# Sixteen projection pieces beside block 0's expert groups, a first tile routed in three parts, and nine row buffers in a kernel that gathers experts

## The chip, the cores and the metric

The kernel runs on one core of one Trainium2 chip. The metric is the device time of one launch in microseconds (us). The engines are named as in the profile: PE (TensorE, matmul), PEld (its weight loads), DVE (VectorE), ACT (ScalarE), POOL (GpSimd) and SP (SyncE, which issues plain transfers). Sixteen DMA engines move data for the core. All values are float32.

## The reference, cut to what matters

A residual block over 1024 tokens of width 1024: two kinds of attention with projections, then a layer that picks, for every token, 128 of 16384 single-neuron experts and sums them.

```python
proj = rmsnorm(h, ln) @ w_in                 # qa, ka, va, qb, kb, vb
o_a = stick_breaking_attention(qa, ka, va)   # group A: 8 heads, all earlier tokens
o_b = sliding_window_sink_attention(rope(qb), rope(kb), vb, sinks)   # group B
h = h + concat(rmsnorm(o_a, sb_norm), rmsnorm(o_b, swa_norm)) @ w_out
t = rmsnorm(h, ln_ffn)
q = (t @ w_query).reshape(tokens, 8, 2, 64)            # 8 routing heads
s = einsum('thpd,hpnd->thpn', q, sub_keys)             # scores of 2 x 128 sub-keys
s1, i1 = top_k(s[:, :, 0], 16); s2, i2 = top_k(s[:, :, 1], 16)
top_s, pos = top_k(s1[..., :, None] + s2[..., None, :], 16)    # 16 experts of a head
g = softmax(top_s)
act = gelu(einsum('thkd,td->thk', expert_u[idx], t))
out = h + einsum('thk,thkd->td', g * act, expert_v[idx])       # then one last rmsnorm
```

## The kernel before, in words

The tokens are cut into eight tiles of 128 (NT). A tile t has a *routing part* (window attention, output projection, norm, query, key scores, top 16, which experts) and a *block* t, in which its experts are fetched and summed. A block has 128 gathers (K): gather k brings, for each of 128 tokens, one row of 2048 values (the expert's two vectors, 8 KB) into one of NB row buffers, `uv[:, slot, :]` in `r_uv`. Two gathers make a *group*; a block has 64 groups (NG). For a group, DVE forms two dot products (L1246), ACT takes their gelu (L898) and builds two scaled identities in place (L901), PE adds the rows into two banks of PSUM (L1577, eight matmul instructions of the profile for a group), and its last matmuls raise `rows_used`, which lets POOL issue the next gather into that buffer (L680).

Every engine works through its own list in order. What a list holds besides the groups is set by tables: `at` gives the group beside which each step of the next tile's routing stands, `at_own` the steps of the block's own tile, `at0` the steps of tile 0 before the first block. A *top* step finds the 16 best keys of both halves of one head (L1061 to L1073), *scores* and *numbers* lay out the candidates (L1136), a *pick* finds one head's 16 experts (L1061 to L1174), a *gate* makes the indices that POOL waits for (`idx_ready`, L1045), *routed* finishes the softmax that the first group of these heads waits for.

The *head* of the program (all before the first gather) holds the norm, the transposes, the value projections, and then the *pieces*: a piece is the projection of one weight chunk (a pair of heads of QA, KA or QB) for 256 tokens, 16 matmul instructions of the profile at L1345 in `sum_piece`; ACT takes it out of PSUM (L756, `keep_piece`), SP stores it in DRAM (`store_piece`). A QB piece is also *turned* by one more matmul (L1359) and roped by DVE (L978 to L980). There are 48 pieces; the head has 42 of them (NH), one to a step s, and between them tile 0's routing and the first twelve units of stick-breaking attention (`first_...`, steps 12 to 19). Pieces 26 to 41 stand after a gap (GAP), in which PE forms tile 0's queries (L1526) and key scores (L1534). The last six pieces stand beside groups 0 to 5 of block 0.

All pieces read the normalised input `xnT`, which lies where row buffers 0 to 3 are; buffers 0 and 1 open when the head's last piece is summed, buffers 2 and 3 after the last piece of all. So the list of slots uses six buffers for groups 0 to 8 and eight from there. The later units of stick-breaking attention (`late_...`) stand beside the groups of blocks 0 to 4 from group 28 on: scores, then four groups later `late_later` (L1375 to L1381), then `late_weigh` (L1388). Between them POOL adds up what the next unit subtracts (`late_add`, L642 and L644), in its own list between two gathers.

## Time and profile before

| | us |
|---|---|
| three runs | 3050.13, 3052.65, 3055.52 (median 3052.65) |
| span of the profiled execution, first to last instruction | 3048.5 |
| what lies around the span, against the median | 4.15 |
| first gather issued / last gather issued | 350.5 / 3019.3 |
| busy in the span: PE, DVE, ACT, POOL | 2245.9, 2188.7, 1151.6, 1317.4 |
| moved in the span | 1143.41 MB, of which the gathers 1073.81 MB |

The profile is of one execution. The page cuts the span into 40 slices of 76 us and gives for each the busy share of the engines in tenths, the mean busy share of the 16 DMA engines and the bytes per second that they moved. The views of stretches give the same for any stretch. Views in order of time give single instructions, with the idle time of the engine before them and what ended it.

### The profile page before, as it was taken

To read this page: it belongs to the slowest core of one execution; us is meant where nothing else is said; L and a number is where in the kernel's file an instruction comes from. 1 tells how busy PE (TensorE), PEld (TensorE's weight loads), DVE (VectorE), ACT (ScalarE), POOL (GpSimd) and SP (SyncE) were. 2 spreads that over 40 slices of the span, in tenths; PEclk is the share of its full clock that TensorE was granted. 3 is DMA by queue.
4 is the path that set the end of the run, shared out by engine and by line. 5 is a ranking of instruction groups with operands and counts; after the bars stand their busy time and mean duration, and the time that the engine had idled before them with its cause. 6 is when DMAs were issued, how large, how long until landed. Compare 5 with 4: busy or idle time off the path is not lost.

```text
span 3048.5 us, 29992 instructions
## 1 busy us (share of the span) xinstructions
PE 2245.9 (74%) x8606; PEld 913.2 (30%) x8606; DVE 2188.7 (72%) x5399; ACT 1151.6 (38%) x2656; POOL 1317.4 (43%) x1134
## 2 busy tenths in 40 slices
PE   8999887786777777776878678876755576555555
PEld 5677733221332123221332124222311132111111
DVE  2121867888788777887788778887777787776654
ACT  4142132774246432663367334753311322121111
POOL 1000144554455444554455544554444444444443
PEclk9999998898889788898899888988877898777777
DMA  3541599999999999999999999999999999999997
GB/s 121 184 129 41 173 388 417 409 407 418 415 418 402 418 413 418 408 415 412 417 406 411 411 416 418 407 398 419 416 415 421 413 404 419 415 420 410 420 420 319
DMA packets 198050, 1143.41 MB, mean 375 GB/s; under 512 B 23584, under 2 KB 55664, under 8 KB 66560
## 3 DMA queue, kind: packets, MB, share of 16 engines
q0 software_dynamic: 147456, 1073.81, 85.7%
q1 hardware_dynamic: 50432, 67.71, 6.6%
q8 instruction: 69, 1.13, 0.1%
q14 instruction: 93, 0.76, 0.1%
HBM read 1126.34 MB, written 15.07 MB: 374 GB/s over the span
## 4 chain that ended last, share of the span: by engine, by line
DMA 35%; PE 29%; DVE 18%; ACT 7%; issue 7%; POOL 4%; SPq 0%; POOLq 0%; ACTq 0%; DVEq 0%
DMA r_uv<-in_experts,r_wk 34%; PE ps L1577 13%; DVE r_uv L1246 8%; PE ps L1345 4%; POOL r_uv L680 4%; PE ps L1509 3%; PE ps L1300 3%; ACT r_uv L901 2%; PE ps L1526 1%; ACT L898 1%; PE ps L1375 1%; DVE r_wk L1173 1%; DVE r_wk L1171 1%; DVE r_wk L1174 1%; ACT r_wk L811 1%
## 5 line engine op out<-in xcount | busy, mean ns | idle before, releaser
L1577 PE MATMUL ps<-r_uv 128*64 128x512 f32 x4096 | 1293.0, 766 | 757.7 <-ACT r_uv L901 735.0
L680 POOL DMA_INDIRECT r_uv<-in_experts,r_wk x1024 | 1207.7, 1179 | 1488.9 <-PE ps L1577 1127.3
L1246 DVE CUSTOM_DVE_ANT_0 r_uv<-r_uv,hnrep 128x1024 f32<-128x1024 f32 x1024 | 1267.0, 1250 | 531.3 <-DMA r_uv<-in_experts,r_wk 516.8
L1577 PEld LDWEIGHTS ps<-r_uv 128*64 128x64 f32 x4096 | 299.1, 162 | 1556.2 <-ACT r_uv L901 1065.9
L898 ACT ACTIVATE r_wk<-r_wk 128x2 f32<-128x2 f32 x512 | 104.1, 203 | 1517.3 <-DVE r_wk L1246 1484.6
L901 ACT ACTIVATE r_uv<-gid,r_wk 128x64 f32<-128x64 f32 x684 | 200.6, 340 | 11.7 <-ACT r_wk L898 0.3
L898 ACT ACT_TABLE_LOAD x136 | 174.5, 1283 | 2.4
L702 ACT ACT_TABLE_LOAD x128 | 164.2, 1283 | 5.7 <-PE ps L1500 1.4
L1526 PEld LDWEIGHTS ps<-r_wk,r_wq 128*128 128x128 f32 x1024 | 124.5, 199 | 57.1 <-issue 57.1
L1526 PE MATMUL ps<-r_wk,r_wq 128*128 128x128 f32 x1024 | 135.4, 288 | 0.8 <-ACT r_wk L840 0.8
L1369 PE MATMUL ps<-r_wk 64*128 64x256 f32 (+2 forms) x384 | 112.3, 414 | 8.8 <-DMA r_wk<-lkv_dram 4.9
L1509 PE MATMUL ps<-r_wo,r_wk 128*128 128x512 f32 x256 | 117.6, 603 | 0.0
L1231 DVE TENSOR_TENSOR gid<-cst,r_wk 128x128 f32<-128x128 f32 x342 | 111.4, 326 | 0.2 <-DVE r_wk L1073 0.2
L1375 PE MATMUL ps<-r_wk,cst 128*128 128x512 f32 (+2 forms) x192 | 106.2, 636 | 5.4 <-POOL r_wk L644 3.0
L901 ACT ACTIVATE r_uv<-cst,r_wk 128x64 f32<-128x64 f32 x340 | 99.7, 340 | 5.8 <-ACT r_wk L898 0.2
L1345 PE MATMUL ps<-r_uv,hnrep 128*128 128x256 f32 x416 | 95.7, 385 | 0.0
L644 POOL TENSOR_TENSOR r_wk<-r_wk 128x512 f32<-128x512 f32 (+1 forms) x64 | 84.3, 1318 | 1.2 <-PE ps L1381 0.2
L1246 DVE DVE_READ_ACCUMULATOR2_ANT r_wk<- 128x1 f32 x1024 | 83.3, 81 | 0.0
L1345 PEld LDWEIGHTS ps<-r_uv,hnrep 128*128 128x128 f32 x416 | 79.1, 192 | 13.7 <-issue 3.0
L1300 PE MATMUL ps<-r_wq,r_wo 128*128 128x512 f32 (+3 forms) x288 | 80.1, 436 | 0.0
L642 POOL COPY r_wk<-r_wk 128x256 f32<-128x256 f32 x32 | 16.9, 529 | 137.9 <-PE ps L1378 121.3
L1381 PE MATMUL ps<-r_wk,cst 128*128 128x512 f32 (+2 forms) x160 | 75.9, 556 | 0.0
(152 smaller groups left out, 2083.1 us busy)
## 6 DMA issues: line engine op xcount, KB each, us to landing
r_uv<-in_experts,r_wk POOLq DMA_INDIRECT x1024
r_wk<-lkv_dram SPq DMA_DIRECT2D x72, 128.0 KB
hnrep<-in_w_chunks SPq DMA_DIRECT2D x14, 512.0 KB, 3.8
r_uv<-in_x SPq DMA_DIRECT2D x8, 512.0 KB, 3.3
r_wo<-in_w_out SPq DMA_DIRECT2D x8, 512.0 KB, 5.2
r_wk<-in_x SPq DMA_DIRECT2D x8, 512.0 KB
r_wq<-in_w_query SPq DMA_DIRECT2D x8, 512.0 KB, 4.2
result<-h2cur SPq DMA_DIRECT2D x8, 512.0 KB
```

What stands on the lines that cost most here:

```text
L680: g.indirect_dma_start(uv[:, SLOT[G], :], None, experts, bass.IndirectOffsetOnAxis(idx[b % 2][:, k:k + 1], 0)).then_inc(rows_in[SLOT[G]], 16)
L702: a.preload_act_table_set("natural_log_exp_and_others")
L898: link(a.activation(actv[:, GRP * n:GRP * n + GRP], actv[:, GRP * n:GRP * n + GRP], ACT.Gelu))
L901: a.activation(uv[:, SLOT[K * b + k], 0:HALF], gid[(NG * b + n) % 3][:, k % GRP, :], ACT.Copy, scale=actv[:, k:k + 1]).then_inc(diag_ready, 1)
L1246: v.tensor_tensor_reduce(uv[:, slot, 0:D], uv[:, slot, 0:D], hnrep[:, k % GRP, :], 1.0, 0.0, ALU.mult, ALU.add, actv[:, k:k + 1]).then_inc ...
L1300: last = t_.matmul(ps[0:rows, bank, 0:w], xTc[:, u, c, 0:rows], wv[:, c, c0:c0 + w], start=c == 0, stop=c == DC - 1)
L1345: last = t_.matmul(ps[:, place, 0:GW], w[:, c, :], xnT[:, tb, c, :], start=c == 0, stop=c == DC - 1)
L1369: t_.matmul(bank(u, r, c0)[:, h, :], k[rows, 0:r], q[rows, c0:GW], start=h == 0, stop=False, skip_group_check=True).then_inc((lz_half, lz_ ...
L1375: last = t_.matmul(bank(u, r, c0), negtri[0:r, 0:r], sp[0:r, :, c0:GW], start=False, stop=not own and rest == GW, skip_group_check=True)
L1509: last = t_.matmul(ps[:, 2 + i, :], (oa, ob)[i // 2][:, c, :], wout[:, 4 * (i // 2) + c, 512 * (i % 2):512 * (i % 2) + 512], start=c == 0, ...
L1526: last = t_.matmul(ps[:, 4 + h // 4, P * (h % 4):P * (h % 4) + P], wq[:, c, P * h:P * h + P], hnT[:, c, :], start=c == 0, stop=c == DC - 1)
L1577: last = t_.matmul(ps[HALF * j:HALF * j + HALF, i, :], uv[:, slot, 0:HALF], uv[:, slot, D + 512 * i:D + 512 * i + 512], start=n == 0, stop ...
```

## The change

- NH falls from 42 to 32: sixteen pieces (all of QA and KA for tokens 512 to 1023) stand beside groups 0, 1, 4, 5, 8, 9, 20, 21, 33, 34, 38, 39, 43, 44, 48 and 49 of block 0. They share one new weight buffer of 4 KB a partition, `stream_chunk`, loaded eight times, seven of these within block 0; before, the last three chunks were loaded once each, ahead of the first gather.
- In the head the twelve QB pieces of tokens 256 to 1023 now come ahead of the gap, in steps 12 to 23, beside the first attention units; they were behind it. Six pieces are left behind the gap, where there were sixteen.
- Tile 0 is routed in three parts: heads 0 and 1, heads 2 and 3, heads 4 to 7. The first gathers wait for two heads where they waited for four. Top steps 3 to 5 and picks 2 and 3 move from the head to block 0 (`own_first`); top steps 6 and 7 stood there before. Routing steps of tile 1 stand up to four groups later (`at_first`).
- Nine row buffers. Buffers 8, 0, 4, 5, 6, 7, 1 serve the first 52 groups; 2 and 3 join at group 52 (WIDE). The 12 KB a partition that the ninth buffer and `stream_chunk` take come from the descriptor scratch of POOL's transfers, cut from 16 KB (the default) to 4 KB.
- PSUM banks of turned and weighed pieces are shared, so some waits are new: a turn waits for the rope of the one before, and the seventh attention unit's weighing waits for two copies of the first pairs (`oa_first`).
- POOL's `late_add` of a unit that starts at group G stands behind the gathers of group G+8 in block 0 as before, and of G+9 in blocks 1 to 4.

```diff
-NB = 8
+NB = 9
-GAP = (26, 32)
+GAP = (26, 29)
+STREAM_GROUPS = (0, 1, 4, 5, 8, 9, 20, 21, 33, 34, 38, 39, 43, 44, 48, 49)
+PARTS = [((0, 2), (2, 4), (4, 8))] + [((0, 4), (4, 8))] * (NT - 1)
+WIDE = 52
+RING = [8, 0, 4, 5, 6, 7, 1]
+for _G in range(NT * K):
+    if _G == GRP * WIDE:
+        _free = [2, 3] + _free
+    SLOT.append(_free.pop(0))
+    _free.append(SLOT[-1])
...
-            opens = {1: (q_roped, len(TURNED)), 2: (proj_summed, NH), NARROW: (proj_summed, NP)}
+            opens = {0: (proj_summed, NQ), 6: (q_roped, len(TURNED)), 1: (proj_summed, NH), 2: (proj_summed, NP)}
+
+            def add_group(b, late, u):
+
+                return min(NG - 1, LATE_AT[late][u] + LATER + (4 if b == 0 else 5))
...
-            at0 = {8: "exp", 10: "pT", 11: "ob", 21: "oa", 22: "r2", 24: "h2sq", 26: "hnT", 43: "gexp"}
+            at0 = {8: "exp", 10: "pT", 11: "ob", 21: "oa", 22: "r2", 24: "h2sq", 26: "hnT", NS: ("gexp", 0)}
...
+            own_first = {0: [("top", 3)], 1: [("scores", 1), ("numbers", 1)], 2: [("pick", 2)], 4: [("pick", 3)],
+                         5: [("gate", 1)], 6: [("top", 4)], 7: [("routed", 1), ("top", 5)], 9: [("top", 6), ("top", 7)],
...
             def first_weigh(u):
...
+                if u == len(FIRST_UNITS) // 2:
+
+                    gate(pe, "pe", oa_first, 2)
...
-                    if b == 0 and n < NP - NH:
-                        sum_piece(NH + n)
+                    if b == 0 and n in STREAM_AT:
+                        sum_piece(STREAM_AT[n])
...
-    nc = bacc.Bacc("TRN2", target_bir_lowering=False, num_devices=1)
+    nc = bacc.Bacc("TRN2", target_bir_lowering=False, num_devices=1, dynamic_dma_scratch_size=4096)
```

Where the change moves instructions, three places. First PE around tile 0's queries and key scores (L1526 and L1534 before are L1577 and L1588 after; L1345 is L1388, a turn L1359 is L1402). Before:

```order
L1509 MATMUL ps<-r_wo,r_wk 128x512 x8
L1345 MATMUL ps<-r_uv,hnrep 128x256 x32
L1516 MATMUL ps<-cst,r_wk 128x128 x8
L1526 MATMUL ps<-r_wk,r_wq 128x128 x64
L1534 MATMUL ps<-keysT,r_wk 128x128 x16
L1345 MATMUL ps<-r_uv,hnrep 128x256 x8
L1345 MATMUL ps<-r_uv,h2cur 128x256 x16
L1359 MATMUL ps<-fnb,cst 128x256
```

and after:

```order
L1388 MATMUL ps<-r_uv,h2cur 128x256 x8
L1567 MATMUL ps<-cst,r_wk 128x128 x8
L1577 MATMUL ps<-r_wk,r_wq 128x128 x40
L1588 MATMUL ps<-keysT,r_wk 128x128 x8
L1577 MATMUL ps<-r_wk,r_wq 128x128 x24
L1588 MATMUL ps<-keysT,r_wk 128x128 x8
L1388 MATMUL ps<-r_uv,hnrep 128x256 x16
L1388 MATMUL ps<-r_uv,h2cur 128x256 x8
L1388 MATMUL ps<-r_uv,hnrep 128x256 x16
L1388 MATMUL ps<-r_uv,h2cur 128x256 x8
L1634 MATMUL ps<-r_uv 64x512 x4
```

The key scores of heads 0 to 3 now come after five of eight queries, and behind the key scores stand six pieces and no turn ahead of the first expert group (L1634).

Second, POOL's gathers at the start of block 0, with what they wait for (L680 before, L715 after). Before:

```order
L680 DMA r_uv<-in_experts,r_wk 128x2048 [waits side_out,v_out,lw_used,idx_ready,rows_used]
L680 DMA r_uv<-in_experts,r_wk 128x2048 [waits rows_used]
L680 DMA r_uv<-in_experts,r_wk 128x2048 [waits q_roped,rows_used]
L680 DMA r_uv<-in_experts,r_wk 128x2048 [waits rows_used]
L680 DMA r_uv<-in_experts,r_wk 128x2048 [waits proj_summed,rows_used]
L680 DMA r_uv<-in_experts,r_wk 128x2048 [waits rows_used] x13
```

and after:

```order
L715 DMA r_uv<-in_experts,r_wk 128x2048 [waits side_out,v_out,lw_used,idx_ready]
L715 DMA r_uv<-in_experts,r_wk 128x2048 [waits proj_summed]
L715 DMA r_uv<-in_experts,r_wk 128x2048 x2
L715 DMA r_uv<-in_experts,r_wk 128x2048 [waits q_roped]
L715 DMA r_uv<-in_experts,r_wk 128x2048
L715 DMA r_uv<-in_experts,r_wk 128x2048 [waits proj_summed]
L715 DMA r_uv<-in_experts,r_wk 128x2048 [waits rows_used] x25
```

Seven gathers stand ahead of the first that waits for a used buffer, and their waits on pieces are on ones that come early, but for the seventh, which waits for the head's last piece.

Third, PE at groups 32 to 34 of block 0 (an expert group is L1577 before and L1634 after; late units are L1369 to L1381 before, L1412 to L1424 after). Before:

```order
L1577 MATMUL ps<-r_uv 64x512 x4
L1375 MATMUL ps<-r_wk,cst 128x2x128
L1378 MATMUL ps<-cst 128x2x128
L1369 MATMUL ps<-r_wk 128x256
L1577 MATMUL ps<-r_uv 64x512 x4
L1375 MATMUL ps<-r_wk,cst 128x512
L1378 MATMUL ps<-cst 128x2x128
L1381 MATMUL ps<-r_wk,cst 128x2x128
L1369 MATMUL ps<-r_wk 16x256
L1577 MATMUL ps<-r_uv 64x512 x4
```

and after:

```order
L1634 MATMUL ps<-r_uv 64x512 x4
L1418 MATMUL ps<-r_wk,cst 128x2x128
L1421 MATMUL ps<-cst 128x2x128
L1412 MATMUL ps<-r_wk 128x256
L1634 MATMUL ps<-r_uv 64x512 x4
L1388 MATMUL ps<-r_uv,stream_chunk 128x256 x8
L1418 MATMUL ps<-r_wk,cst 128x512
L1421 MATMUL ps<-cst 128x2x128
L1424 MATMUL ps<-r_wk,cst 128x2x128
L1412 MATMUL ps<-r_wk 16x256
L1634 MATMUL ps<-r_uv 64x512 x4
L1388 MATMUL ps<-r_uv,stream_chunk 128x256 x8
```

A piece stands between an expert group and the late unit's matmuls at eight of the groups from 33 to 49.

## Rows read from the trace of the kernel before

**Rows 1.** The page, slices of the span: DMA busy tenths, bytes moved

```profile
DMA  3541599999999999999999999999999999999997
GB/s 121 184 129 41 173 388 417 409 407 418 415 418 402 418 413 418 408 415 412 417 406 411 411 416 418 407 398 419 416 415 421 413 404 419 415 420 410 420 420 319
```

**Rows 2.** The page, queues: packets, MB, share of 16 engines' span

```profile
q0 software_dynamic: 147456, 1073.81, 85.7%
q1 hardware_dynamic: 50432, 67.71, 6.6%
```

**Rows 3.** Stretches: length, engines' busy us, granted clock, DMA share, GB/s

```profile
350.00:434.00 84.00, 68.26 (x291) 40.45 (x290) 61.89 (x184) 21.91 (x67) 32.08 (x28) 0.92 0.92 348
434.00:543.00 109.00, 85.28 (x391) 39.53 (x391) 88.01 (x233) 37.70 (x94) 51.18 (x42) 0.90 1.01 418
543.00:634.00 91.00, 73.70 (x268) 24.52 (x266) 75.58 (x168) 65.18 (x117) 51.98 (x44) 0.89 1.00 402
617.00:3030.00 2413.00, 1698.25 (x6178) 576.33 (x6177) 1871.01 (x4527) 937.13 (x2195) 1179.11 (x1003) 0.84 1.01 413
...
580.00:590.00 10.00, 9.86 (x42) 3.15 (x40) 8.25 (x22) 7.83 (x17) 6.02 (x5) 0.99 0.93 360
...
3020.00:3030.00 10.00, 5.20 (x16) 1.17 (x16) 5.34 (x10) 1.60 (x7) 0.21 (x1) 0.83 0.89 368
```

**Rows 4.** PE in the head, in order of time: start, length, instructions

```profile
125.25 3.62 PE L1345 MATMUL ps<-r_uv,h2cur 128*128 128x256 f32 x16
...
129.14 3.62 PE L1345 MATMUL ps<-r_uv,hnrep 128*128 128x256 f32 x16
...
222.03 0.66 PE L1388 MATMUL ps<-r_uv 128*64 128x128 f32 x8
...
267.11 13.98 PE L1345 MATMUL ps<-r_uv,hnrep 128*128 128x256 f32 x64
...
280.92 1.04 PE L1516 MATMUL ps<-cst,r_wk 128*128 128x128 f32 x8
...
282.79 7.38 PE L1526 MATMUL ps<-r_wk,r_wq 128*128 128x128 f32 x64 [0.83 <-ACT r_wk L840]
...
297.24 2.82 PE L1534 MATMUL ps<-keysT,r_wk 64*128 64x128 f32 x32
```

**Rows 5.** DVE and POOL from tile 0's first top step to the first gather

```profile
299.72 0.49 DVE L1061 MAX8 r_wk<-r_wk 128x8 f32<-128x128 f32 x2 [20.01 <-ACT r_wk L849]
...
302.73 0.49 DVE L1061 MAX8 r_wk<-r_wk 128x8 f32<-128x128 f32 x2
...
316.90 0.78 DVE L1136 TENSOR_TENSOR r_wk<-r_wk 128x64 f32<-128x64 f32 x7
...
341.06 0.42 DVE L978 TENSOR_TENSOR r_uv<-ps,r_uv 128x256 f32<-128x256 f32 x1
...
342.42 0.21 DVE L1061 MAX8 r_wk<-r_wk 128x8 f32<-128x50 f32 x1
...
346.21 0.99 DVE L1174 TENSOR_REDUCE r_wk<-r_wk 128x16 f32<-128x800 f32 x1
...
348.74 0.74 DVE L1045 CAST r_wk<-r_wk 64x32 uint32<-64x32 f32 x4
...
350.53 1.20 POOL L680 DMA_INDIRECT r_uv<-in_experts,r_wk  x1 [122.95 <-issue]
```

**Rows 6.** The first groups: DVE's dots, PE's sums, POOL's next issue

```profile
363.00 2.79 DVE L1054 COPY hnrep<-r_wk 64x1024 f32<-64x1024 f32 x4
365.83 1.22 DVE L1246 CUSTOM_DVE_ANT_0 r_uv<-r_uv,hnrep 128x1024 f32<-128x1024 f32 x1
...
377.65 1.22 DVE L1246 CUSTOM_DVE_ANT_0 r_uv<-r_uv,hnrep 128x1024 f32<-128x1024 f32 x1
...
379.94 0.28 DVE L1231 TENSOR_TENSOR gid<-cst,r_wk 128x128 f32<-128x128 f32 x1
...
381.61 1.94 PE L1577 MATMUL ps<-r_uv 128*64 128x512 f32 x8
...
384.35 0.94 POOL L680 DMA_INDIRECT r_uv<-in_experts,r_wk  x1 [2.27 <-PE ps L1577]
```

**Rows 7.** POOL's gathers: ns least, median, most; first and last start

```profile
L680 POOL DMA_INDIRECT r_uv<-in_experts,r_wk x1024: 932/949/2612, 350.5 to 3019.3; - x171
```

More of the change, by code:

```diff
@@ L683, in gathers_of @@
                     if late is not None and k % GRP == GRP - 1:
[L684 to L685 removed]
+                        for u in range(len(LATE[late][1])):
+                            if add_group(b, late, u) == k // GRP:
+                                late_add(b, late, u)
             for b in range(NT):
@@ L1529, in tile_step @@
                 elif step[0] == "keys":
+                    if t == 1 and step[1]:
+                        gate(pe, "pe", proj_kept, NH + sum(n < 29 for n in STREAM_GROUPS))
                     pe.wait_ge(qT_kept, 2 * t + 1 + step[1])
```

266 lines of the change are left out of this document (144 added, 122 removed).

## Prediction, on record before the changed kernel ran

> **What bounds the kernel now.** I read the slices first. From the sixth slice on the DMA line shows 9, and 400 to 420 GB/s are moved [rows 1]. The queues say by whom: the gathers' packets fill 85.7% of sixteen engines' span, 0.857 x 3048.5 = 2613 us, or 2.55 us for each of 1024 gathers, and the plain transfers 6.6%, 201 us [rows 2]. The stretches show that nothing else counts in between: from 617 to 3030 the DMA share is 1.01, while PE is busy 1698 of 2413 us and DVE 1871 [rows 3]. So the time is the moment of the first gather, plus what the DMA engines must move after it, plus the time in which they have nothing to do, plus a short end. Of such holes there are few. Cut into 260 stretches of 10 us from 430 to 3030, the trace has 21 with a share under 1.00 (the first and the last in [rows 3]); what they lack against the usual 1.015 adds up to 10.7 us. The stretch from 350 to 434 has a share of 0.92, so 84 x 0.095 = 8 us of holes. Everything that the change can win lies in the first 350 us and in these 19 us.
>
> **The head.** Three edits move the first gather. (1) The twelve QB pieces now come ahead of tile 0's queries, and each brings a turn. A piece with a turn takes 129.14 - 125.25 = 3.89 us, one without 13.98 / 4 = 3.50 [rows 4]; 12 x 0.4 = 4.7 us on PE, which has no idle time there. The ropes lie on DVE beside it. (2) The weighing at 222.03 [rows 4] now waits for two pairs of copies, which stand on DVE behind the rope of the turn just done: a rope takes 342.42 - 341.06 = 1.4 us [rows 5], the copies about 0.9, so 2.5 us (0 to 4) in which PE and all behind it wait. Together the transpose at 280.92 moves to 288.1. (3) The first key scores come after five queries, not eight: 282.79 to 297.24 is 14.45 us for eight [rows 4], so 5.4 us less. They start at 297.2 + 7.2 - 5.4 = 299.0, and the first top step 2.5 us later, as now (299.72 after 297.24), at 301.5. From there DVE alone decides: two top steps of 3.0 (299.72 to 302.73), scores and numbers of two heads some 2.3 (0.78 for the four heads' scores), two picks of 4.8 (342.42 to the end of the reduce at 347.2), the indices 0.9, and 1.0 from there to the issue [rows 5]: 6.0 + 2.3 + 9.6 + 0.9 + 1.0 = 19.8. The eight ropes that stood between these steps are gone. First gather at **321.3** instead of 350.5: **29 us won** (25 to 33).
>
> **The first stretch.** What is late next is the first dot. PE finishes the second half of queries and key scores at about 308 and six pieces of 3.5 us at 329; ACT takes the last piece out and forms the gates' exponential only then (both stand at the end of its head), so DVE, done with top step 2 at 323, waits to 329.6. With 1.4 us for the gates and 2.8 for the copies of the normed rows [rows 6] the first dot starts at about 334, 12.6 us after the first issue; now it is 15.3. Seven gathers are under way by then, 17.9 us of moving, to about 341; the first buffers come free at 334 + 2.5 for two dots + 4.4 (379.94 to 384.35) [rows 6] = 341, and the next gather moves some 2 us later. After this DVE sets the pace: ten groups need 10 x 2.5 of dots and identities (377.65 to 380.15, [rows 6]), top steps 3 to 7 15.0, picks 2 and 3 9.6, and mask, candidates, gates and a copy some 9, together 59 us. DMA needs 20 x 2.55 = 51 plus about 7 for stores, three weight chunks and a window. That is level, with jitter: I take 8 us of holes, as now (3 to 18), so **0**.
>
> **More bytes behind the first gather.** Seven loads of 0.524 MB and some seven more stores of 0.131 MB: 4.6 MB. The gathers pay 2613 / 1073.8 = 2.43 us for a MB, the plain queue 201 / 67.7 = 2.97 [rows 2]; small stores are the dearer kind. 11 to 14, **12 us**, all on the path.
>
> **Seven buffers until group 52, and PE beside them.** Now eight serve from group 9. With eight, 434 to 543 has a share of 1.01 [rows 3]; a buffer less takes one gather, 2.55 us, from the lead. I take 5 us (0 to 10). Groups 33 to 49 are the tight place. PE is busy 73.7 of 91 us from 543 to 634 [rows 3], which are about these groups; eight pieces add 8 x 3.5 = 28, to 102. DMA has 91 plus 8 for its own share of the pieces: 99. Also, `late_add` of a unit that starts at group G comes behind a gather that now waits for group G+5's sums, one group later than with eight buffers; the next unit's matmuls, beside that same group if it started at G+1, then wait for an issue and an addition, about 2.5 us. Where a piece stands between (groups 33, 39, 48) it hides this, at 36, 42 and 45 nothing does. So PE needs 102 to 109 against 99: another 5 us (2 to 15). Together **10 us** (2 to 25).
>
> **Nine buffers from group 52 on.** They can give back holes only, some 9 of the 10.7 us, as the rest is the end of the gathers and what block 0 has. A lead longer by 2.55 us closes most holes of 1 us or less: **6 us won** (0 to 9). The later additions of blocks 1 to 4 fall on a PE that idles 30% of the time [rows 3]: nothing.
>
> **The smaller scratch.** What shows in the trace: 147456 packets for 1024 gathers [rows 2], 144 each, nine to an engine, and never more than nine gathers open, 81. The Trainium skill (DMA: Bandwidth & Descriptors, "The descriptor swizzle") has nine read and nine write descriptors per engine for such a transfer and 16 bytes for one ("Terms"); 4096 / 16 = 256, room for 28 gathers, is an estimate from that page, and by it the cut costs nothing. No run here shows that size yet. I take 0 (0 to 9, the price of slower issues below).
>
> **The sum.** -29 + 0 + 12 + 10 - 6 = -13 us. Span 3048.5 - 13 = 3035.5; the median of the runs is 4.15 above the span, so 3039.5, **3039 us**.
>
> **Rivals.**
> - *Block 0 keeps up.* DVE and PE are not the limit anywhere and the ninth buffer closes all holes: -29 + 12 - 4 - 9 = -30, 3022 us. For it: the DMA work of the new pieces widens every group. Against it: DVE's 59 against 58.
> - *The gain is given back in block 0.* The first stretch runs 3 us worse and groups 28 to 52 cost 20: -29 + 3 + 12 + 20 - 6 = 0, 3052 us. For it: PE's 102 to 109 against 99, in lists worked in order with a shorter lead.
> - *Slower: PE at its lower clock.* The mechanism is the pieces at half speed. The granted clock is 0.90 and 0.89 of full in 434 to 634 [rows 3], that is, part of the time PE is at 1.2 GHz, after waits for ACT. If the pieces fall into that, each takes 7 us: eight are 56, PE needs 130 in groups 33 to 49 against 99, 31 us lost; -29 + 12 + 31 + 5 - 6 = +13, 3065 us. It turns slower from about 25 us lost in block 0, six of the eight pieces at the low level. Against it: a PE with more to do waits less.
> - *The ninth buffer does nothing.* The holes come from something that a longer lead doesn't reach: 3045 us.
> - *POOL is slowed by DVE.* Issues take 949 ns in the median, up to 2612 [rows 7], 1179.11 us busy for 1003 of them [rows 3], so 0.23 us each over the median, hidden by the lead. With an empty queue, as in the first 40 gathers, the lengthening is on the path: 40 x 0.23 = 9 us, 3048 us. The Trainium skill (SBUF — State Buffer, "Who interferes with whom") gives a rule for this: some copies on DVE lock POOL out of the port with which it writes descriptors. By that rule moving top steps and copies beside gathers lengthens issues; that some are longer agrees, that it costs time is not seen.
>
> **How the numbers follow.** The forecast has 0.50, block 0 keeping up 0.13, given back 0.17, slower 0.10, the idle ninth buffer 0.06, POOL 0.04. A measurement of this kernel can tell about 0.2%, 6 us, from no change. Faster by more: nearly all of the forecast, block 0 keeping up, and most of the idle ninth buffer, 0.68. Within: given back, POOL and the edges, 0.21. Slower: 0.11. The range reaches from the best case, 3022, to just over the given-back one, 3054; the bounds of the terms (25 to 33, 11 to 14, 2 to 25, 0 to 9, 3 to 18 for 8) add up to about the same.
>
> **What would show it.** The first gather at 321 (318 to 326), the first dot 12 to 13 us behind it, DVE idle ahead of it for 6 us. A DMA share of 0.9 in the first 84 us behind the first gather, near 1.01 and at worst 0.95 in groups 28 to 52, and hardly a stretch of 10 us under 0.99 after group 52. PE busy over 90% in groups 33 to 49, with waits for POOL at L1418. Wrong I would be if the first gather were later than 326, if PE's clock fell under 0.85 beside the pieces, or if the gathers' rate behind group 52 changed at all apart from the holes.

## The result, and the profile after

The changed kernel takes **3090.3 us** (median of four runs, 3088.7 to 3094.9), the kernel before, beside it, 3054.1 us. The ratio is 1.0123, with a 95% interval of 1.0111 to 1.0135: slower by 1.2%, where 3039 us and a small gain were forecast. The profiled execution has a span of 3089.9 us, 41.4 us more than the 3048.5 of before; it is the one that is taken apart here. The medians lie 36.2 us apart. Around the span of the changed kernel lie 1.8 us (3091.7 against 3089.9), so of the 4.15 us of the kernel before some 2 are that its profiled execution was quicker than its median.

The page of the changed kernel, first the DMA share and the bytes by slice, then the two queues, then the line of PE's `late_later` matmuls (name, count, busy us and mean ns, idle us ahead of them and who ended it):

```profile
DMA  3532799889999999999999999999999999999997
GB/s 119 185 120 64 298 404 401 329 349 419 418 418 417 417 413 418 402 418 416 411 384 380 371 418 418 362 367 414 418 420 419 419 404 419 416 420 410 419 420 319
...
q0 software_dynamic: 147456, 1073.81, 84.9%
q1 hardware_dynamic: 51584, 71.90, 6.9%
...
L1418 PE MATMUL ps<-r_wk,cst 128*128 128x512 f32 (+2 forms) x192 | 114.2, 680 | 79.3 <-POOL r_wk L675 73.3
```

and the same line of the kernel before:

```profile
L1375 PE MATMUL ps<-r_wk,cst 128*128 128x512 f32 (+2 forms) x192 | 106.2, 636 | 5.4 <-POOL r_wk L644 3.0
```

Against [rows 1], where the GB/s line stands between 398 and 421 from the seventh slice to the last but one, there are three dips: 329 and 349 (540 to 695 us, the late groups of block 0), 384, 380, 371 (1545 to 1776 us, block 3) and 362, 367 (1931 to 2085 us, block 4). Between them the rate is what it was. And a wait has grown from 3.0 us: PE idles 79.3 us ahead of L1418, 73.3 of it for POOL L675. L675 is the addition in `late_add`, L1418 the first matmul of `late_later`.

The same as stretches (length, busy us of each engine, granted clock, DMA share, GB/s): the first groups behind the first dot, the middle of block 0, its late groups, and the halves of blocks 3 and 4 with late units.

```profile
344.00:424.00 80.00, 59.15 (x244) 30.10 (x246) 75.38 (x238) 23.28 (x72) 29.54 (x27) 0.88 1.00 400
424.00:545.00 121.00, 101.51 (x472) 51.80 (x469) 98.90 (x275) 51.04 (x112) 53.88 (x44) 0.94 0.99 398
545.00:660.00 115.00, 100.95 (x380) 45.15 (x380) 72.34 (x160) 68.17 (x125) 50.18 (x46) 0.90 0.86 317
1557.00:1745.00 188.00, 139.22 (x478) 44.33 (x476) 148.79 (x353) 120.10 (x214) 104.17 (x84) 0.87 0.94 369
1911.00:2098.00 187.00, 144.80 (x466) 45.55 (x466) 143.36 (x344) 117.21 (x208) 98.97 (x83) 0.84 0.95 372
```

PE is busy 0.84 of the second stretch, 0.88 of the third and 0.74 and 0.77 of the last two; no engine is full, and yet the DMA engines have holes. A *hole* is counted here and below from the packets: the share of the sixteen engines that moves nothing, added up over a stretch and given in us.

When gathers number 0, 16 and so on have their last packet in, after against before, worked out from both traces' packets (two gathers make a group, 128 a block):

| gather | before, us | after, us | difference | with late_add back (e_add34) | head mended too (e_head34) |
|---|---|---|---|---|---|
| 0 | 356.6 | 336.2 | -20.5 | -17.9 | -31.7 |
| 16 | 412.3 | 383.7 | -28.5 | -25.5 | -38.9 |
| 64 | 538.3 | 519.0 | -19.3 | -13.5 | -28.1 |
| 104 | 646.4 | 658.7 | +12.2 | -2.2 | -15.0 |
| 128 | 707.7 | 721.4 | +13.6 | -0.8 | -13.7 |
| 448 | 1546.1 | 1557.0 | +10.9 | -3.8 | -17.1 |
| 512 | 1716.6 | 1744.5 | +27.9 | -4.0 | -15.5 |
| 576 | 1883.4 | 1911.4 | +28.1 | -4.6 | -15.7 |
| 640 | 2054.6 | 2097.3 | +42.7 | -5.0 | -19.1 |
| 1023 | 3032.6 | 3075.8 | +43.1 | -1.2 | -16.2 |

So 17 us are lost in the second half of block 3 (gathers 448 to 512), 15 in that of block 4, 42 in block 0 behind gather 16; 28.5 are won up to there and 3 in blocks 1 and 2, and 43 are left. These halves are where the late units start, in blocks 0, 3 and 4 two in three groups; blocks 1 and 2, whose units start two groups apart, lose nothing. PE's waits for POOL at L1418 lie in the same places: 14.9 us in block 0, 5.5 in blocks 1 and 2, 58.7 in blocks 3 and 4.

What a late unit waits for, from the changed kernel's trace of block 3, PE and POOL in order of time (start, length, line, what ended the idle time ahead):

```profile
1611.64 1.94 PE L1634 MATMUL ps<-r_uv 128*64 128x512 f32 x8
...
1614.69 1.67 POOL L715 DMA_INDIRECT r_uv<-in_experts,r_wk  x1 [2.70 <-issue]
1616.38 1.27 POOL L675 TENSOR_TENSOR r_wk<-r_wk 128x512 f32<-128x512 f32 x1
...
1617.79 2.04 PE L1418 MATMUL ps<-r_wk,cst 128*128 128x512 f32 x2 [4.22 <-POOL r_wk L675]
1617.81 1.75 POOL L715 DMA_INDIRECT r_uv<-in_experts,r_wk  x1 [0.16 <-issue]
...
1619.63 1.91 PE L1424 MATMUL ps<-r_wk,cst 128*128 128x512 f32 x2
```

PE ends a group's sums at 1613.6, and only then may POOL issue the gather which stands ahead of the addition in its list (it waits for `rows_used`, which these sums raise). The issue starts at 1614.7 and takes 1.67 us, the addition 1.27, and PE, with the next unit's `late_later` at its head, stands idle for 4.22 us. The next group's sums, which would free the next buffers, are queued behind it. And the two groups of matmuls that follow take 2.04 and 1.91 us, where the unit at 1608.5, behind a wait of 0.2 us, takes 1.10 and 1.02: the granted clock from 1617 to 1620 is 0.50, the lower level of 1.2 GHz. It isn't so behind every wait. Of the 18 waits for POOL at L1418 that are longer than 3 us, 15 are followed by matmuls that run at the lower clock at least in part, three (3.2, 3.4 and 3.6 us) by ones at the full clock; of the 19 shorter waits, one is followed by slower ones.

The head. PE in order of time, changed kernel:

```profile
222.87 3.72 PE L1388 MATMUL ps<-r_uv,hnrep 128*128 128x256 f32 x16
...
229.91 1.12 PE L1431 MATMUL ps<-r_uv 128*64 128x128 f32 x8 [2.89 <-DVE r_wk L1065]
...
230.96 2.08 PE L1418 MATMUL ps<-r_wk,cst 128*128 128x512 f32 x2
...
237.44 3.72 PE L1388 MATMUL ps<-r_uv,hnrep 128*128 128x256 f32 x16
...
296.17 1.09 PE L1567 MATMUL ps<-cst,r_wk 128*128 128x128 f32 x8 [2.15 <-DVE r_wk L1161]
298.10 10.80 PE L1577 MATMUL ps<-r_wk,r_wq 128*128 128x128 f32 x80 [0.83 <-ACT r_wk L876]
308.82 1.71 PE L1588 MATMUL ps<-keysT,r_wk 64*128 64x128 f32 x16
```

The transpose stands at 296.2, not at the 288.1 of the prediction; the first gather was issued at 330.5.

### The profile page after: what moved, and what is told of

Same layout as the page of the kernel before. It is cut to its first block, busy times and chain, and to the rows that moved or that the text cites. A ratio compares the mean times of both kernels' runs of the same rounds, so it can differ in the third digit from the quotient of the medians.

```text
span 3089.9 us, 30050 instructions
## 1 busy us (share of the span) xinstructions
PE 2238.4 (72%) x8606; PEld 913.6 (30%) x8606; DVE 2183.6 (71%) x5428; ACT 1152.0 (37%) x2659; POOL 1332.8 (43%) x1134
## 3 DMA queue, kind: packets, MB, share of 16 engines
q8 instruction: 69, 1.13, 0.1%
## 4 chain that ended last, share of the span: by engine, by line
PE 36%; DMA 33%; DVE 14%; ACT 7%; issue 6%; POOL 4%; SPq 0%; POOLq 0%; ACTq 0%; DVEq 0%
DMA r_uv<-in_experts,r_wk 32%; PE ps L1634 15%; DVE r_uv L1285 6%; PE ps L1388 5%; POOL r_uv L715 3%; PE ps L1560 3%; PE ps L1337 3%; PE ps L1418 2%; ACT r_uv L940 2%; PE ps L1577 2%; PE ps L1424 2%; POOL r_wk L675 1%; PE ps L1412 1%; ACT L937 1%; ACT r_wk L847 1%
## 5 line engine op out<-in xcount | busy, mean ns | idle before, releaser
L715 POOL DMA_INDIRECT r_uv<-in_experts,r_wk x1024 | 1230.5, 1202 | 1506.8 <-PE ps L1634 1197.2
L1634 PE MATMUL ps<-r_uv 128*64 128x512 f32 x4096 | 1256.9, 747 | 733.9 <-ACT r_uv L940 712.9
L1634 PEld LDWEIGHTS ps<-r_uv 128*64 128x64 f32 x4096 | 294.3, 160 | 1524.3 <-ACT r_uv L940 1033.9
L1418 PE MATMUL ps<-r_wk,cst 128*128 128x512 f32 (+2 forms) x192 | 114.2, 680 | 79.3 <-POOL r_wk L675 73.3
L1577 PEld LDWEIGHTS ps<-r_wk,r_wq 128*128 128x128 f32 x1024 | 123.9, 199 | 47.7 <-issue 47.6
L1577 PE MATMUL ps<-r_wk,r_wq 128*128 128x128 f32 x1024 | 134.1, 288 | 0.8 <-ACT r_wk L876 0.8
L1412 PE MATMUL ps<-r_wk 64*128 64x256 f32 (+2 forms) x384 | 113.1, 419 | 3.5 <-DMA r_wk<-lkv_dram 2.4
L841 ACT ACTIVATE r_wk<-ps 128x512 f32<-128x512 f32 (+2 forms) x84 | 47.5, 565 | 111.0 <-PE ps L1424 108.7
L1424 PE MATMUL ps<-r_wk,cst 128*128 128x512 f32 (+2 forms) x160 | 88.2, 637 | 0.0
L1388 PE MATMUL ps<-r_uv,hnrep 128*128 128x256 f32 x352 | 82.8, 391 | 0.0
L675 POOL TENSOR_TENSOR r_wk<-r_wk 128x512 f32<-128x512 f32 (+1 forms) x64 | 76.5, 1195 | 1.2 <-PE ps L1424 0.3
## 6 DMA issues: line engine op xcount, KB each, us to landing
r_uv<-in_experts,r_wk POOLq DMA_INDIRECT x1024, 14.1
```

Source lines behind the costliest of these rows:

```text
L715: g.indirect_dma_start(uv[:, SLOT[G], :], None, experts, bass.IndirectOffsetOnAxis(idx[b % 2][:, k:k + 1], 0)).then_inc(rows_in[SLOT[G]], 16)
L1388: last = t_.matmul(sums, w[:, c, :], xnT[:, tb, c, :], start=c == 0, stop=c == DC - 1)
L1418: last = t_.matmul(bank(u, r, c0), negtri[0:r, 0:r], sp[0:r, :, c0:GW], start=False, stop=not own and rest == GW, skip_group_check=True)
L1424: last = t_.matmul(bank(u, r, rest), negones[:, 0:r], acc[:, :, rest:GW], start=False, stop=True, skip_group_check=True)
L1577: last = t_.matmul(ps[:, 4 + h // 4, P * (h % 4):P * (h % 4) + P], wq[:, c, P * h:P * h + P], hnT[:, c, :], start=c == 0, stop=c == DC - 1)
L1634: last = t_.matmul(ps[HALF * j:HALF * j + HALF, i, :], uv[:, slot, 0:HALF], uv[:, slot, D + 512 * i:D + 512 * i + 512], start=n == 0, stop ...
```

## Experiments

Each kernel ran beside the kernel before, and the ratio to it stands with each time. A single trace can lie some us off the median of its kernel (e_head34: 3032.4 in the profiled execution, 3040.2 in the median), so small differences go by the times, places by the traces. The ratio isn't that of the two medians. Where a price is given as a range, one end is the difference of the medians and the other that of the ratios.

**e_add4: late_add back in its place in blocks 1 to 4.**

```
-                return min(NG - 1, LATE_AT[late][u] + LATER + (4 if b == 0 else 5))
+                return min(NG - 1, LATE_AT[late][u] + LATER + 4)
```

> The changed kernel, and only in blocks 1 to 4 each late_add stands one group earlier again (behind the gathers of group G+8, where it waits for the sums of group G+4, as with eight buffers); block 0 is as in the changed kernel. Theory A (the later place of late_add is what costs: PE's next late_later, at L1418, waits for a gather issue and an addition on POOL): the 17 us that gathers 384 to 512 lost and the 15 us that gathers 512 to 640 lost come back, 3090 - 32 = 3058 us, between 3052 and 3064; the waits of PE for POOL L675 fall from 73 us to about 35; block 0 still ends some 13 us late. Theory B (the blocks 3 and 4 lose it by the ninth buffer itself or by the descriptor scratch of 4 KB, PE's waits are a sign and not the cause): 3085 to 3092 us.

Measured: 3062.1 us, ratio 1.0023 (1.0014 to 1.0033), 28 us under the changed kernel by the medians, 31 by the ratios. The waits for POOL fell to

```profile
PE ps L1418 <- POOL r_wk L675: 12.7, 6, 3.3
```

(us in all, times, longest), and the stretch that took 188 us takes 176, at 395 instead of 369 GB/s:

```profile
1557.00:1733.00 176.00, 136.55 (x482) 43.56 (x481) 143.43 (x353) 121.22 (x215) 103.60 (x85) 0.90 0.99 395
```

One digit of one line is worth 28 of the 36 us. Theory B falls. But the waits fell to 12.7 us where 35 were expected: block 0, which is left as it was, holds 14.9 us of them in the changed kernel, not half of the 73.

**e_add34: the same in block 0.**

```
+                return min(NG - 1, LATE_AT[late][u] + LATER + (3 if b == 0 and LATE_AT[late][u] + LATER + 3 < WIDE else 4))
```

> As e_add4, and in block 0, where seven buffers serve, late_add stands one group earlier as well (behind the gathers of group G+7, from which they wait for group G+4; for the few units whose place would lie in or past group 52 the place stays). Theory A: block 0 lost 39 us between gathers 40 and 104; the waits for POOL at L1418 in block 0 are about half of the 73 us, and when they go PE has 8 x 3.5 = 28 us more to do than before in groups 33 to 49 but no more; I expect 20 us (10 to 30) back, so 3058 - 20 = 3038 us, between 3028 and 3050. Rival C (block 0 loses by the load of the pieces on PE and by the buffer less, not by the waits): no more than 5 us under e_add4.

Measured: 3047.9 us, ratio 0.9966 (0.9951 to 0.9981): 14 us less than e_add4 by the medians, 17 by the ratios, 16 between the two traces, and the kernel is now faster than the one before. Rival C had no more than 5. The expected 20 (10 to 30) rested on half of the 73 us of waits; it came near with 14.9 us, because in block 0 a wait costs about its whole length. The late groups of block 0 then run with PE nearly full and at full clock:

```profile
545.00:645.00 100.00, 94.25 (x398) 44.18 (x394) 75.41 (x168) 71.02 (x129) 51.75 (x47) 1.00 0.97 382
```

**b_add_later: the kernel before, with late_add one group later.**

```
-                        for u in late_units(late, k // GRP - NB // GRP - LATER):
-                            late_add(b, late, u)
+                        for u in range(len(LATE[late][1])):
+                            if min(NG - 1, LATE_AT[late][u] + LATER + 5) == k // GRP:
+                                late_add(b, late, u)
```

> The kernel before, with one edit: each late_add stands one group later, behind the gathers of group G+9, where with eight buffers it waits for the sums of group G+5. Theory A: PE waits for POOL in the units one group apart, in blocks 3 and 4 as in the changed kernel (+32 us), in block 0 without the pieces less than there (+5 to +20): 3054 + 32 + 12 = 3098 us, between 3080 and 3110, with about 60 us of waits at L1375 for L644. Theory B: within 5 us of 3054.

Measured: 3171.0 us, ratio 1.0391 (1.0359 to 1.0423). The direction is as theory A has it, the size is not: +117 us, not +44. The trace of this kernel has

```profile
PE ps L1376 <- POOL r_wk L644: 163.1, 58, 5.6
...
PE ps L1376 <- POOL r_wk L642: 17.0, 6, 3.7
```

180 us of waits, and block 3 loses 43 us, block 4 40, block 0 31. With eight buffers the gather ahead of the addition waits for the second gather of group G+5, with nine for the first, and the lead that can absorb the wait is a gather shorter. This account of the size is argued, no run tries it alone. What a us of wait costs differs by block:

| PE's waits for POOL, us, and what the stretch loses | block 0 | blocks 1 and 2 | blocks 3 and 4 |
|---|---|---|---|
| changed kernel | 14.9, loses 14 to 17 | 5.5, loses nothing | 58.7, loses 28 to 32 |
| b_add_later | 42, loses 31 | 40, loses 3 | 98, loses 83 |

In blocks 1 and 2, whose units start two groups apart, even 40 us of waits cost next to nothing; where units start one group apart they cost half of their length or more.

**e_one34: e_add34 with one eighth of the streamed pieces' matmuls.**

```
-                for c in range(DC):
+                deep = DC if i < NH else 1
+                for c in range(deep):
...
-                                     stop=c == DC - 1)
+                                     stop=c == deep - 1)
```

> As e_add34, and the sixteen streamed projection pieces do one of their eight matmuls each, so that queries and keys of tokens 512 to 1023 are wrong; all loads, copies, ropes and stores stay. It takes 16 x 7 x 0.43 = 48 us off PE, 24 us of it in groups 33 to 49. If PE's load is what block 0 still loses by (rival C), it ends 10 to 20 us under e_add34, about 3025 us; if the waits for late_add were all (theory A), it ends within 4 us of e_add34.

Measured: 3045.2 us, ratio 0.9965 (0.9951 to 0.9979), against 0.9966. 48 us of work taken off PE move next to nothing (2.7 us by the medians, 0.3 by the ratios): by itself, PE's load was not what block 0 still lost by.

**e_head34: e_add34 with three places on DVE and ACT changed in the head.**

```
-            at0 = {8: "exp", 10: "pT", 11: "ob", 21: "oa", 22: "r2", 24: "h2sq", 26: "hnT", NS: ("gexp", 0)}
+            at0 = {8: "exp", 10: "pT", 11: "ob", 21: "oa", 22: "r2", 23: "h2sq", 26: "hnT", NS: ("gexp", 0)}
...
-            at0 = {7: "mask", 9: "norm", 10: "pT", 23: "r2", 24: "h2", 25: "hn", 28: ("top", 0), 29: ("top", 1),
+            at0 = {7: "mask", 9: "norm", 10: "pT", 22: "r2", 25: "hn", 28: ("top", 0), 29: ("top", 1),
...
+                if s == 23:
+                    tile_step("h2", 0)
                 if s - 2 in PIECE_AT and PIECES[PIECE_AT[s - 2]][0] == QB:
                     rope_piece(PIECE_AT[s - 2])
...
-                if c in (5, 8):
-                    dve.wait_ge(lw_used, len(FIRST_UNITS) * (c - 2) // 6)
-                    first_out(2 * (c // 3) - 2)
-                    first_out(2 * (c // 3) - 1)
+                if c in (4, 8):
+                    dve.wait_ge(lw_used, len(FIRST_UNITS) * (c // 4) // 2)
+                    first_out(2 * (c // 4) - 2)
+                    first_out(2 * (c // 4) - 1)
```

> The kernel of the run e_add34, and in the head: the two copies of first_out that a weighing waits for stand on DVE one step earlier, ahead of the softplus pair; the polish r2 and the step h2 of tile 0 stand ahead of the rope of the turn that PE only reaches behind the output projection; ACT squares h2 one step earlier. The trace of the changed kernel has PE idle 2.9 us before 229.91 for these copies, about 1.9 us more by the lower granted clock right behind it, and 2.15 us before 296.17 for hn. Theory D (these DVE places are two thirds of the excess of the head over the predicted 288.1): the transpose hnT starts 6 to 7 us earlier, near 290, the first gather near 325, and the time is 3048 - 6 = 3042 us. Rival E (PE has no slack behind, the turns themselves cost): within 2 us of e_add34, the first gather at 330.

Measured: 3040.2 us, ratio 0.9960 (0.9945 to 0.9974). PE in this kernel's head:

```profile
219.90 3.72 PE L1390 MATMUL ps<-r_uv,hnrep 128*128 128x256 f32 x16
...
223.98 0.66 PE L1433 MATMUL ps<-r_uv 128*64 128x128 f32 x8
...
229.91 3.72 PE L1390 MATMUL ps<-r_uv,hnrep 128*128 128x256 f32 x16
...
286.61 1.09 PE L1569 MATMUL ps<-cst,r_wk 128*128 128x128 f32 x8
288.53 9.17 PE L1579 MATMUL ps<-r_wk,r_wq 128*128 128x128 f32 x80 [0.83 <-ACT r_wk L876]
297.63 1.71 PE L1590 MATMUL ps<-keysT,r_wk 64*128 64x128 f32 x16
```

The waits are gone, the weighing takes 0.66 us instead of 1.12, from one piece to the next it is 10.0 us instead of 14.6, five queries take 9.17 instead of 10.80, and the transpose stands at 286.6. The first gather was issued at 319.3. That is more than the 6 to 7 us of theory D, and it is not luck of one trace: the six kernels with this head have it at 318.9 to 323.5 (319.3, 319.2, 318.9, 320.4, 321.4, 323.5), the six with the changed kernel's head at 327.0 to 333.0. In the time of the whole, though, the medians are 8 us apart and the ratios 0.0006, with intervals that overlap. That the first gather is some 10 us sooner is shown; that the kernel is faster by as much is not. With the additions back and the head mended the kernel takes what was forecast for the change, 3039 us, and that is luck in part: by the trace the head gives 31 us (29 predicted), the first stretch 7 (0), block 0 takes 25 (22), and what comes behind it gives 2 (6).

**e_fo34: only first_out's place.** The edit is the last hunk above.

> The kernel of the run e_add34, and of the head's edits only the first: the copies of first_out for which a weighing waits stand one step earlier on DVE, ahead of the softplus pair. In three runs with the wait the piece behind it began 16.0 us after the piece before it (222.85 to 238.85), in e_head34 10.0 us. Theory D: the idle 2.9 us and the lower granted clock that follows it are one cause, so this edit alone gives 4.5 to 6 us, and the piece stands 10 us behind: 3048 - 5 = 3043 us, hnT near 291 to 292. Rival: the rest of e_head34's gain was h2's place, and this run gives 2 to 3 us: 3045.5 us.

Measured: 3043.7 us, ratio 0.9965 (0.9954 to 0.9976). The piece stands 10.0 us behind the one before it (223.58, 233.59), the transpose at 292.3, the first gather at 325.0. So a wait of 2.9 us had cost 4.6 to 6 us, with the lower clock behind it (0.61 granted from 229 to 233 in the changed kernel, 1.00 from 223 to 230 in e_head34), and the place of r2 and h2 gives the other 5.7 us at the transpose.

**e_wide54, e_wide64: when the chunk's two buffers join.** `WIDE = 52` becomes 54 (on e_add34) and 64 (on e_head34).

> The kernel of the run e_add34, with the two buffers of the chunk joining at group 54 instead of 52. In e_add34 the gather of group 52 was issued 14.7 us behind that of group 51, waiting 6.3 us for PE L1388, the last streamed piece (it stands in group 49), and the DMA share from 620 to 640 was 0.86. Theory F: the join at 52 is a wait of its own, about 3 us: 3045 us and no such gap. Rival: seven buffers for four gathers more cost the same; 3048 us.

Measured: 3045.6 us, ratio 0.9974 (0.9965 to 0.9983), against 0.9966: the gap at the join is gone from the trace (no holes between gathers 96 and 112, where e_add34 has 3.4 us). The medians lie 2 us apart and the ratios the other way, so the time is the same; the trace has its holes a few groups earlier.

> The kernel of the run e_head34, with seven buffers for all of block 0: the two of the chunk join at group 64, not 52. It prices seven buffers. The recorded prediction takes 5 us (0 to 10) for the whole of block 0's narrow part. Theory: with late_add in its place seven serve at a share of 0.97 to 1.0, so twelve groups more cost 2 us and the wait of 6 us at the join goes: within 3 us of 3040. Rival (seven buffers are what makes block 0 slow, 24 gathers more at the 2.66 us of gathers 40 to 104 against 2.59 of eight): 3 to 6 us slower, 3045.

Measured: 3040.7 us, ratio 0.9962 (0.9949 to 0.9976), against 0.9960. Gathers 104 to 128 go at 2.69 us with seven buffers and 2.61 with nine, 2 us in all.

**e_eight34: e_add34 with eight buffers from group 52.** `_free = [2, 3] + _free` becomes `_free = [2] + _free`.

> The kernel of the run e_add34, but one buffer, not two, joins at group 52: eight buffers serve from there, as in the kernel before. From gather 128 to the last e_add34 took 2324.5 us and the kernel before 2324.9, with 12.8 and 11.4 us of DMA holes: by these the ninth buffer gives nothing once late_add is back in its place, and this run is within 3 us of e_add34 (3045 to 3051). By the recorded prediction (the ninth buffer closes holes, 6 us) it is 3054 us.

Measured: 3049.8 us, ratio 0.9988 (0.9978 to 0.9997), against 0.9966. From gather 128 to the last its trace takes 2326.3 us, that of e_add34 2324.5. The ninth buffer is worth 2 us by the trace and the medians, 7 by the ratios; the prediction's 6 lies within.

**b_scratch: the kernel before with the smaller descriptor scratch.** `dynamic_dma_scratch_size=4096` is added, nothing else.

> The kernel before, with the descriptor scratch of 4 KB and nothing else. The recorded prediction has 0 (0 to 9) for it: 3054 us, with issues of 949 ns in the median as before. If the smaller scratch made issues longer or wait, the backlog of the gathers hides up to about 6 us of it each, and the time is up to 3063 us.

Measured: 3053.8 us, ratio 1.0002 (0.9993 to 1.0011). The gathers' issues (least, median, most ns, first and last start) are as in [rows 7]:

```profile
L680 POOL DMA_INDIRECT r_uv<-in_experts,r_wk x1024: 932/960/2808, 352.0 to 3025.9; - x171
```

The scratch costs nothing here. The Trainium skill (DMA: Bandwidth & Descriptors, "The descriptor swizzle") led to the same answer by its count of descriptors.

**e_noload and e_light: the new loads, and loads and matmuls together.** Both are e_head34 without the seven loads; e_light has also the edit of e_one34.

```
                             gate(e, "sp", proj_summed, i + 1)
-                            load_chunk(c + 1)
...
-                    gate(pe, "pe", stream_in, 16 * (c - TAIL + 1))
+                    gate(pe, "pe", stream_in, 16)
```

> The kernel of the run e_head34, without the seven loads of weight chunks behind the first gather: all sixteen streamed pieces are formed with the first chunk's weights, so queries and keys of tokens 512 to 1023 are wrong. SP still waits where it did. It prices the term of the new bytes: by the recorded prediction 4.6 MB cost 12 us, of which the loads are 3.67 MB, some 9.5 us: 3040 - 9.5 = 3030.5. In the traces block 0 loses 17 to 18 us between gathers 16 and 128 beside the holes; if the loads hit thin queues, they are worth more, 14 us, 3026. If they run in the holes, less than 5 us.

Measured: 3035.9 us, ratio 0.9938 (0.9925 to 0.9952): 4 to 7 us for 3.67 MB, where the prediction's price gives 9.5. In the trace block 0 is no shorter without them (322.4 us from gather 16 to 128, against 320.7 in e_head34). The plain transfers take 8 us less of the sixteen engines there, but holes come in their place: 17.7 us up to gather 128, with the loads 10.0.

> The kernel of the run e_head34, with both of the things left out that e_one34 and e_noload left out one at a time: the sixteen streamed pieces do one of eight matmuls each and the seven later chunk loads are gone, so queries and keys of tokens 512 to 1023 are wrong; the copies on ACT, the stores and all waits stay. Each alone changed the time from gather 16 to 128 by 1 to 2 us of the 25 us that block 0 loses against the kernel before. Theory G (the loads and the matmuls cover each other, each alone would do): with both gone block 0 gets 10 us or more back, 3030 us or less. Theory H (seven buffers limit block 0: 6.1 open gathers against 7.5, whatever PE and the loads do): within 3 us of e_noload, 3033 to 3039.

Measured: 3031.5 us, ratio 0.9923 (0.9909 to 0.9936): 9 to 11 us under e_head34. Theory H (within 3 us of e_noload) is off by a little, theory G holds in part. Its one trace has 317.7 us from gather 16 to 128, 3 less than e_head34's and not 10, so this rests mostly on the times.

**e_early: the pieces ten groups sooner, nine buffers from group 42.** On e_head34, `WIDE = 42` and

```
-STREAM_GROUPS = (0, 1, 4, 5, 8, 9, 20, 21, 33, 34, 38, 39, 43, 44, 48, 49)
+STREAM_GROUPS = (0, 1, 4, 5, 8, 9, 11, 13, 20, 21, 23, 25, 33, 34, 36, 37)
```

> The kernel of the run e_head34, with the sixteen streamed pieces at groups 0, 1, 4, 5, 8, 9, 11, 13, 20, 21, 23, 25, 33, 34, 36 and 37, and nine buffers from group 42 instead of 52. In e_one34 PE's load was taken away and the time stayed, so the pieces' place is worth little to PE; the loads and stores of the chunks move into the first 30 groups, where seven buffers and DVE's routing leave thin queues, and the ninth buffer comes ten groups sooner. Theory: -3 us from the join (no wait for L1388 at the join, fewer thin groups), 0 from PE: 3037 us, between 3034 and 3042. Rival: the first stretch is too tight for two more loads and loses what the join gives: 3041 to 3045.

Measured: 3043.8 us, ratio 0.9969 (0.9957 to 0.9981). The rival holds: between gathers 64 and 128 it loses 5.9 us to the kernel before where e_head34 loses 14.4, and between 16 and 64 it loses 19.1 where that loses 10.8.

**b_seven and b_seven_late: seven buffers in block 0 of the kernel before.** Both cap the open gathers of groups 9 to 51 at seven; b_seven also puts late_add one group earlier there.

```
-                    gate(pool, "pool", rows_used, G + (3 if 6 <= G < GRP * NARROW else 1))
+                    gate(pool, "pool", rows_used, G + (3 if 6 <= G < GRP * NARROW else 2 if 6 <= G < 104 else 1))
```

> The kernel before, with seven instead of eight gathers open in groups 9 to 51 of block 0 (each of these gathers waits for the release of the gather seven before it), and late_add there one group earlier, so that it waits for group G+4 as before. No streamed pieces. Theory H: gathers 18 to 103 go at some 2.85 us instead of 2.62, as in the runs with seven buffers: 86 x 0.2 = 17 us, 3070 us. Theory G: seven buffers without pieces cost what the groups 52 to 63 showed in e_wide64 (2.69 us a gather against 2.61), 86 x 0.08 = 7 us: 3060 us. The recorded prediction: 5 us for it.

Measured: 3059.4 us, ratio 1.0017 (1.0008 to 1.0026): seven buffers cost 5 to 6 us (the trace loses 5.0 between gathers 16 and 128), near theory G's 7 and what the prediction took. Theory H's 17 falls.

> As b_seven, but late_add stays at group G+8, where with seven gathers open it waits for group G+5, as in block 0 of the changed kernel. It prices that wait in block 0 alone, without pieces. e_add4 against e_add34 had it at 14 us with pieces; theory A: 10 to 20 us over b_seven, about 3080 us. If pieces were needed for it to matter: within 3 us of b_seven.

Measured: 3064.7 us, ratio 1.0035 (1.0021 to 1.0049). Here the late addition costs 5 us in block 0, without pieces, less than the 10 to 20 of theory A; with them it was 14. The waits themselves are alike (16.3 us in block 0 here, 14.9 in the changed kernel). That they cost more beside the pieces is measured; why isn't.

**e_sooner: late_add at G+7 in all blocks.** On e_head34, `LATER + 3` throughout.

> The kernel of the run e_head34, with late_add behind the gathers of group G+7 in all blocks, also where nine buffers serve, so that it stands ahead of the sums it waits for less and POOL itself waits for ltri_done of the unit, which PE makes in group G+4 right behind the sums. If PE's remaining waits for POOL (2 us at a time) still cost something in blocks 1 to 4: 3038 us. If POOL then holds back the gather behind the addition, so that the lead is that of eight buffers: 3040 to 3044 us. It tells whether G+4 is the edge: one group later cost 32 us, one group sooner should cost nearly nothing.

Measured: 3052.1 us, ratio 1.0002 (0.9991 to 1.0012): 12 us slower than e_head34, where at most 4 were expected. PE hardly waits for POOL any more (0.2 us), but now POOL stands at the addition,

```profile
POOL r_wk L675 <- PE ps L1426: 106.8, 40, 7.1
```

and the gather behind it with it; in e_head34 that wait is 17.2 us. The place has an edge on both sides: one group too late costs 28 us in blocks 1 to 4, one too early 12.

## Why the prediction was wrong

**The later additions (predicted: nothing in blocks 1 to 4, a part of 5 us in block 0).** This is the step that failed. The text had the whole mechanism: that `late_add` now stands behind a gather which waits for group G+5, and that the next unit's matmuls then wait for an issue and an addition. It priced it by PE's load: "The later additions of blocks 1 to 4 fall on a PE that idles 30% of the time: nothing". But PE's idle time is no store from which a wait is paid. PE waits at a point where the next group's sums stand behind it, these free the buffers, and the buffers are the whole lead of the gathers. The idle 30% lie at other points, where PE waits for the scaled identities that ACT builds behind the dots. The kernel before:

```profile
L1577 PE MATMUL ps<-r_uv 128*64 128x512 f32 x4096 | 1293.0, 766 | 757.7 <-ACT r_uv L901 735.0
```

Measured: 28 us in blocks 3 and 4 (e_add4), 14 us in block 0 (e_add34), against nothing and a part of 5. The price of one wait, "about 2.5 us", was right: 73.3 us in 35 waits are 2.1 each, 4.3 at most. What was wrong is at how many places it counts; that the matmuls behind most of the long ones run at half clock was missed too.

**The ninth buffer (predicted -6).** 2 to 7 us won, shown by e_eight34. Right in size, hidden under the step above.

**Block 0's buffers and PE (predicted +10), bytes (predicted +12).** Behind gather 16 block 0 lost 42 us. With the additions back in their place (e_add34) the trace still loses 24.7. Its packets between gathers 16 and 128, against the kernel before, say how the DMA engines spend them:

| us of all sixteen engines | before | e_add34 | b_seven |
|---|---|---|---|
| plain transfers | 13.2 | 25.7 | 13.1 |
| gathers' packets | 285.1 | 290.2 | 288.3 |
| holes | 1.5 | 9.0 | 3.3 |

The plain transfers move 4.7 MB more and take 12.5 us for it: the predicted 12, all in block 0, and the plain queue's whole share agrees (0.069 x 3089.9 = 213 against 201, [rows 2]). Seven buffers alone (b_seven) lengthen the gathers' packets by 3.2 and add 1.8 of holes, the predicted 5. The other 7 to 8 us, holes most of them, aren't settled. The stores, the copies on ACT and the routing steps on DVE that now stand among the first groups (DVE is busy 0.94 from 344 to 424, 0.74 in the first stretch of [rows 3]) are what is left, and none of them was tried by itself. That the parts add up like this is an account, not a test. Taking parts out gave back 4 to 7 us for the loads (e_noload), whose share in the 12 was 9.5, nothing clear for the pieces' matmuls (e_one34), and 9 to 11 for both (e_light). The groups 33 to 49 as the tight place of PE, "PE needs 102 to 109 against 99", was a wrong picture. PE is busy 0.88 of that stretch, 0.94 once the waits are gone, and with seven eighths of the pieces' matmuls taken out next to nothing came back.

**The head (predicted -29, measured -20).** The first gather was at 330.5, not 321.3. The transpose moved by 15.2 us (280.9 to 296.2), not 7.2: turns 12 x 0.43 = 5.2 (predicted 4.7), the wait for first_out with what follows it 4.6 (2.5), a wait for hn 2.15, a piece at the lower clock 1.7, and 1.5 by which PE was late already at 185 us. The last is spread between executions: the same piece starts between 183.1 and 186.2 us in the traces of all kernels with the changed tables, none of which differ up to there. Behind it five queries ahead of the key scores saved what was said, but at the lower clock they took 10.80 instead of 9.17; top step to issue 19.2 (19.8). What failed is the wait for `first_out`: the 2.5 us were counted (2.9 measured), the clock behind them was not, and 14.6 us lie between two pieces where 9.6 lay before. And one wait was missed: tile 0's r2 and h2 stand on DVE behind the rope of a turn that PE reaches only after the output projection, so hn comes 2.15 us late for PE. The rest of the head's mechanism was right: with the three places mended, the first gather stands at 318.9 to 321.4 in five of six traces. The predicted 321.3 had 2.5 us for a wait that this head hasn't, so without it the forecast is 318.8.

**The first stretch (predicted 0, 8 us of holes as before).** Mis-sized to the other side: up to gather 16 the trace has 1.4 us of holes where the kernel before has 7.4, and the lead grows from 20.5 to 28.5 us. The first dot came 14.1 us behind the first issue (12.6 predicted), DVE idled 7.5 us for the gates' exponential (6 predicted); the holes of before went with the new routing order by all that the trace shows, but no run tried it by itself.

**The scratch (predicted 0).** Shown by b_scratch.

**The rivals.** "Slower: PE at its lower clock" had the right sign, but not the place: the granted clock from 545 to 660 is 0.90 (0.89 in [rows 3]), and pieces at half clock are not what costs. The lower clock costs in the head and behind most of the long waits for POOL. "POOL is slowed by DVE" is not seen: the first 40 issues, of which it spoke, take 1.13 us in the mean against 1.22 before. No rival had the additions as a cause of their own; the wait was named and put at nothing, and so the range ended 36 us too low.

The sum as measured, span against span: -20 (head) - 8 (first stretch) + 42 (block 0) - 3 (blocks 1 and 2) + 17 + 15 (blocks 3 and 4) and nothing behind them make +43; the span has +41, as 2 us less lie behind the last gather.

## What to carry to other kernels

When one more buffer moves work that is queued behind a gather's wait, count in groups what that gather now waits for: an addition that another engine needs must not stand behind a wait for the very work that this engine does last before it needs the addition. An engine's idle share says nothing on what a new wait costs; ask what stands behind the waiting instruction, and whether it frees the resource that makes the lead. Give such a step a place of its own and try it one to either side: here the places G+7 and G+8 in blocks 1 to 4 give 3052 and 3040 us, and G+9 was 28 us worse than G+8 in the kernel whose head wasn't mended.

## What the runs showed of the hardware that was not expected

- In the head, where PE has hardly any idle time, a wait of PE cost more than its length. The 2.9 us of idle time in the head were followed by matmuls at 1.2 GHz (2.08 us for 1.12, a weighing of 1.12 for 0.66) and cost 4.6 to 6.0 us between two pieces. In `late_later` most long waits do the same (2.04 us for 1.10 behind waits of 3.2 to 4.3 us), but three of 18 over 3 us don't. Beside the gathers the whole effect on the time runs from nothing (blocks 1 and 2) to the wait's full length (block 0).
- The same program's head differs between executions by whole pieces at the lower clock: the piece near 185 us took 3.72 us in some traces and 5.41 in others, without a wait in the row, and the first gather moved by up to 6 us with the same head (327.0 to 333.0 in six traces).
- A descriptor scratch of 4 KB carries the eight open gathers of the kernel before (1.05 MB each) at the same time as the larger one, with issues of 960 ns in the median against 949.
